# Four-layer backbone kernel: the next unit's scores issued ahead of the inverse's last product, three products placed on other quarters of TensorE, and the last layer's r and g computed for latents only

## The reference

```python
def _rwkv7_step(state, inp):
    r, w, k, v, kk, a = inp
    sa = jnp.einsum("dbhvk,dbhk->dbhv", state, kk)
    state = (state * w[..., None, :] - sa[..., None] * (kk * a)[..., None, :]
             + v[..., None] * k[..., None, :])
    return state, jnp.einsum("dbhvk,dbhk->dbhv", state, r)
...
    r, k, v, g = jnp.einsum("nbtd,nde->nbte", xs[:4], w_rkvg)
...
    _, y = lax.scan(_rwkv7_step, s0, (shared(r), to_scan(decay), to_scan(k_dir),
                                      shared(v), shared(kk), to_scan(iclr)))
    y = y.transpose(1, 2, 0, 3, 4)
    y = y[0] + _seg_flip(y[1], n_ctx, 1)
    if not need_ctx:
        y, r, k, v, g = (a[:, n_ctx:] for a in (y, r, k, v, g))
...
    o = (yn + bonus).reshape(bsz, -1, D_INNER) * jax.nn.silu(g.astype(F32))
```

## Time and profile before

| | |
|---|---|
| median of 3 runs | 6824.17 us |
| profiled execution, its own time | 6829.33 us |
| its span in the trace | 6827.5 us, 212950 instructions |
| TensorE matmul busy | 5819.9 us (85%) |
| VectorE busy | 2964.0 us (43%) |
| ScalarE busy | 2007.9 us (29%) |
| GpSimd busy | 1862.0 us (27%) |
| TensorE's instruction packets (queue q8) | 293, 4.80 MB |
| mean granted TensorE clock | 0.923 |

### The profile page before, as it was taken

The page is one execution under the profiler, slowest core; times in us unless marked ns, Lnnn a source line. Parts: engine busy times, 40 slices in busy tenths (PEclk is TensorE's granted clock), DMA queues, the critical chain, the costliest instruction groups (busy, mean ns, idle before and its releaser), DMA issues. The chain is left out here.

```text
span 6827.5 us, 212950 instructions
## 1 busy us (share of the span) xinstructions
PE 5819.9 (85%) x91944; PEld 3913.5 (57%) x91944; DVE 2964.0 (43%) x6321; ACT 2007.9 (29%) x3323; POOL 1862.0 (27%) x2006
## 2 busy tenths in 40 slices
PE   5999788888887799978897984796999788888887
PEld 4555577777774355445553553543555577777773
DVE  6100366666662233145524368323100366666661
ACT  1000244444440222134312232211000345454440
POOL 4452244443431336000003541000000244434340
PEclk8999899999998899989898987898999999999998
DMA  3222100011002222122122337422111100110002
GB/s 122 90 97 82 42 30 30 30 43 38 30 30 88 115 99 81 39 79 74 50 72 105 100 97 77 135 73 85 69 67 66 41 30 30 43 38 30 30 30 89
DMA packets 196079, 443.13 MB, mean 65 GB/s; under 512 B 24768, under 2 KB 108608, under 8 KB 195648
## 3 DMA queue, kind: packets, MB, share of 16 engines
q1 hardware_dynamic: 160896, 338.58, 16.7%
q10 hardware_dynamic: 34752, 98.61, 3.6%
HBM read 329.14 MB, written 107.97 MB: 64 GB/s over the span
## 5 line engine op out<-in xcount | busy, mean ns | idle before, releaser
L356 PE MATMUL ps<-arena 128*128 128x512 f32 (+1 forms) x4672 | 1713.1, 529 | 73.6 <-DMA arena<-s_w_in 27.6
L356 PEld LDWEIGHTS ps<-arena 128*128 128x128 f32 x4672 | 886.9, 190 | 894.6 <-issue 855.3
L1860 PE MATMUL ps<-arena 64*64 64x64 f32 x35840 | 736.6, 224 | 160.1 <-ACT arena L2245 57.8
L153 POOL TENSOR_TENSOR arena<-arena 128x512 f32<-128x512 f32 (+1 forms) x360 | 331.0, 936 | 1779.3 <-DMA arena<-w_mod 1769.1
L1860 PEld LDWEIGHTS ps<-arena 64*64 64x64 f32 x35840 | 642.5, 136 | 245.6 <-issue 228.8
L2245 ACT COPY arena<-ps 128x512 f32<-128x512 f32 (+1 forms) x880 | 536.0, 630 | 531.7 <-PE ps L1860 521.0
L2388 POOL TENSOR_TENSOR arena<-arena 128x256 f32<-128x256 f32 (+1 forms) x320 | 305.3, 961 | 904.2 <-DVE arena L2609 445.8
L570 PE MATMUL ps<-arena 128*128 128x512 f32 (+1 forms) x1152 | 424.3, 528 | 33.3 <-DMA arena<-na_w_in 33.3
L1621 DVE SCALAR_TENSOR_TENSOR arena<-arena 128x1280 f32<-128x1280 f32 (+2 forms) x128 | 152.5, 1265 | 617.1 <-PE ps L356 502.7
L1685 ACT COPY arena<-ps 128x1280 f32<-128x1280 f32 x64 | 78.4, 1225 | 1105.0 <-PE ps L356 775.0
L2313 POOL MEMSET arena<- 128x1280 f32 (+4 forms) x22 | 15.1, 739 | 1423.7 <-POOLq L83 1423.7
(11 more groups left out here) (258 smaller groups left out, 9730.4 us busy)
## 6 DMA issues: line engine op xcount, KB each, us to landing
arena<-proj SPq DMA_DIRECT2D x158, 640.0 KB, 5.1
proj<-arena ACTq DMA_DIRECT2D x96, 640.0 KB, 3.9
arena<-w_mod SPq DMA_DIRECT2D x96, 512.0 KB, 7.6
arena<-rw_w SPq DMA_DIRECT2D x68, 512.0 KB, 3.6
arena<-xres SPq DMA_DIRECT2D x40, 640.0 KB, 7.0
xres<-arena ACTq DMA_DIRECT2D x24, 640.0 KB, 6.1
arena<-na_w_in SPq DMA_DIRECT2D x24, 512.0 KB, 3.5
arena<-x SPq DMA_DIRECT2D x16, 640.0 KB, 6.6
```

Source lines behind the costliest of these rows:

```text
L153: self.nc.gpsimd.tensor_tensor(out, strip[:, c:c + n, :], self.k.cond[:, c:c + n, s:s + 1].to_broadcast([P, n, P]), ALU.mult)
L356: last = nc.tensor.matmul(k.ps[:, 3 * u + n, 0:b - a], w[:, c * P:(c + 1) * P], src[:, c, a:b], start=(c == 0), stop=(c == KT - 1))
L1860: last = PE.matmul(part_of(out, dst, hh, g, d), part(l, src, hh, g, d), rhs, start=True, stop=True)
```

## The change

- *Scores.* x of the next unit is issued between f4 and f5, xt between f5 and gh (`first_scores`, `turned_scores`). They wait for a new semaphore `kk_ready` (BH and KK made), m for `ops_ready`. The fifth unit issues them too, on old operands, and its result isn't used; the first unit of the next group has its scores issued in the turn, behind step 19. The first pair of all stands before the loop. f5 now goes to `low[2]`, since `low[1]` takes xt.
- *Order in a unit.* On TensorE x2 and x2t come first, then transitions, x4, local outputs, f1. VectorE makes BH ahead of zt's copy, KK behind it, R and the mask of x behind the last `eyed`, the mask of xt before it negates half of gh, and the third mask and KH behind that. ScalarE's decays stand between the copies of f1 and f2, and z's copy ahead of kb's. POOL waits for gh before its first `with_eye`.
- *Quarters.* `product` gets `stay`: with 1, f5's results stay in the half from which they are read, so that f5 uses two quarters and gh, which reads them crosswise, four. w goes over four quarters. The four KK transposes become 16 products with the unit matrix.
- *Last layer.* r and g (n = 0 and 3) are mixed, multiplied, copied and stored for the latents only.
- *Fill.* 147 increments behind layer 0's norm, 217 behind layer 3's.

Cut to its core:

```diff
-NORM_FILL = {0: 19, 3: 148}
+NORM_FILL = {0: 147, 3: 217}
...
+    def tokens_of(n):
+
+        return NCTX if last_layer and n in (0, 3) else 0
...
-                            strip_matmuls(nc, k, u, strips_[:, u, :], xs[n % 2]).then_inc(mm_done[u], 1)
+                            strip_matmuls(nc, k, u, strips_[:, u, :], xs[n % 2], chunks_of(n)).then_inc(mm_done[u], 1)
...
-            def product(out, l, r, t):
+            def product(out, l, r, t, stay=0):
...
-                                src, dst = c ^ (hh & t), c ^ (hh & (t + 1))
+                                src, dst = c ^ (hh & t), c ^ (hh & (t + 1 + stay))
...
-            def window(it, late):
-
-                pe.wait_ge(ops_ready, it + 1)
+            def first_scores():
+                scores(low[0], KK_, BH_).then_inc(x_mm, 1)
+
+            def turned_scores():
+                scores(low[1], BH_, KK_).then_inc(xt_mm, 1)
+
+            def window(it, late, scored):
+
+                pe.wait_ge(xt_ev, it + 1)
                 hold(k, pe)
-                scores(low[0], KK_, BH_).then_inc(x_mm, 1)
-                scores(low[1], BH_, KK_).then_inc(xt_mm, 1)
+                product(low[0], A1, A0, 0).then_inc(x2_mm, 1)
+                product(low[3], A0, A1, 0).then_inc(x2t_mm, 1)
...
                     PE.transpose(bank[7][:, g * P:(g + 1) * P], v_win[:, g * P:(g + 1) * P], k.ident)
                     for d in range(2):
-                        last = PE.transpose(bank[6][:, (g * 2 + d) * P:(g * 2 + d + 1) * P], ops[:, KK_, d, g * P:(g + 1) * P], k.ident)
+                        for hh in range(2):
+                            for c in range(2):
+                                at, col = (2 * g + c) * C, (4 + g * 2 + d) * C
+                                last = PE.matmul(bank[6 + hh][HP[c ^ hh], col:col + C], ops[HP[hh], KK_, d, at:at + C], k.eye2[HP[hh], :],
+                                                 start=True, stop=True)
...
-                                last = PE.matmul(part_of(low[3], c, hh, g, d), part(M1, c, hh, g, d), Vt[HP[c], g, HP[hh]],
+                                last = PE.matmul(part_of(low[3], c ^ hh, hh, g, d), part(M1, c, hh, g, d), Vt[HP[c], g, HP[hh]],
...
                 pe.wait_ge(yz4_ev, it + 1)
+                pe.wait_ge(kk_ready, scored + 2)
+                hold(k, pe)
+                first_scores()
                 pe.wait_ge(f4_ev, it + 1)
                 hold(k, pe)
-                product(low[1], Ya, F, 7).then_inc(f5_mm, 1)
+                product(low[2], Ya, F, 7, 1).then_inc(f5_mm, 1)
+                turned_scores()
 
                 pe.wait_ge(f5_ev, it + 1)
                 hold(k, pe)
-                for hh in range(2):
-                    for g, d, q in pairs:
+                for g, d, q in pairs:
+                    for hh in range(2):
                         for c in range(2):
-                            last = PE.matmul(bank[4 + hh][HP[c], q * P:(q + 1) * P], part(F, c, hh, g, d), RH[HP[c], hh * 4 + q, :],
-                                             start=True, stop=True)
+                            last = PE.matmul(bank[4 + hh][HP[c], q * P:(q + 1) * P], part(F, c ^ hh, hh, g, d),
+                                             RH[HP[c ^ hh], hh * 4 + q, :], start=True, stop=True)
...
                 step(19)
+                pe.wait_ge(kk_ready, e * (NW2 + 1) + (NW2 + 2))
+                hold(k, pe)
+                first_scores()
+                turned_scores()
...
                 for n in range(NW2):
+                    if e or n:
+                        pool.wait_ge(gh_mm, e * NW2 + n)
                     with_eye(n, xt_ev, F[:, 0:M // 2], A1[:, 0:M // 2])
...
                     if n + 2 < NW2:
-                        sums(e, n + 2)
+                        sums_scan(e, n + 2)
+                    if more:
+                        operands_beta(e, n + 1)
                     dve.wait_ge(zt_mm, it)
                     V.tensor_scalar(wide(B1), low[1], -1.0, None, ALU.mult).then_inc(zt_ev, 1)
+                    if more:
+                        operands_kk(e, n + 1)
+                    else:
+                        dve.sem_inc(kk_ready, 1)
...
                     eyed(Ya, low[0]).then_inc(yz4_ev, 1)
-                    if n + 1 < NW2:
-                        operands(e, n + 1)
...
+                    if more:
+                        operands_r(e, n + 1)
+                        mask_scores(e, n + 1)
+                    if n + 2 < NW2:
+                        sums_rest(e, n + 2)
+                    if more:
+                        mask_turned(e, n + 1)
```

More of the change, by code:

```diff
@@ L1636, in _ @@
                 dve.drain()
-                for c in range(KT):
-                    last = mix(0, c, a, b)
-                last.then_inc(xs_part, 1)
+                if a >= tokens_of(0):
+                    for c in range(KT):
+                        last = mix(0, c, a, b)
+                    last.then_inc(xs_part, 1)
             for n in range(1, 6):
@@ L1680, in _, with kept @@
         def _(act):
-            with act.Fori(0, 16) as i:
+            def kept(i, first):
                 for u in range(2):
@@ L2493, in operands_rk, with masked, mask_scores, mask_turned @@
                 dve.drain().then_inc(ops_ready, 1)
-            def operands(e, n, first=False):
-                operands_kk(e, n, first)
-                operands_rk(e, n)
+            def masked(out, in_, mask):
+                return V.tensor_tensor(out.rearrange("p (h g q) -> p h g q", h=2, g=2), in_.rearrange("p h (g q) -> p h g q", g=2),
+                                       flat(mask).unsqueeze(1).unsqueeze(1).to_broadcast([P, 2, 2, 2 * C]), ALU.mult)
+            def mask_scores(e, n):
+                dve.wait_ge(x_mm, e * (NW2 + 1) + (n + 1))
+                hold(k, dve)
+                masked(A0, low[0], k.m_x)
+            def mask_turned(e, n):
+                dve.wait_ge(xt_mm, e * (NW2 + 1) + (n + 1))
+                hold(k, dve)
+                masked(A1, low[1], k.m_xt).then_inc(xt_ev, 1)
+            def mask_rest():
+                masked(NT, low[1], k.m_nt).then_inc(nt_ev, 1)
             def centred(e, banks, c):
@@ L2542, in _ @@
                 kk_unit(0, KK_AHEAD, c)
-            operands(0, 0, True)
+            operands_beta(0, 0, True)
+            operands_kk(0, 0)
+            operands_r(0, 0)
+            mask_scores(0, 0)
+            mask_turned(0, 0)
+            mask_rest()
+            operands_keys(0, 0)
             sums(0, 1)
@@ L2703, in _ @@
                 add_backward(4)
+                mask_turned(e + 1, 0)
+                mask_rest()
+                operands_keys(e + 1, 0)
                 sums(e + 1, 1)
```

100 lines of the change are left out of this document (58 added, 42 removed).

## The result

The changed kernel took 6754.01 us, the median of six runs (6732.09 to 6809.95), against 6823.11 us before (6807.96 to 6831.81); the ratio is 0.9914, with a 95% interval of 0.9888 to 0.9941. It is faster by 0.9%; between the medians stand 69 us, half of the 137 us forecast. Its runs lie 78 us apart, those of before 24 us. The profiled execution is the slowest of them, 6809.95 us (span 6808.1), so its parts are read one by one and not as the median's.

The account below looks back on a forecast made before the run. It took each scan unit as one chain on TensorE with short waits that other engines close. Terms -61 - 32 - 55 + 10.5 + 0.5 = -137 us; 6829.3 - 137 - 5.2 = 6687 us (chance 0.50), own range 6610 to 6760, overall 6610 to 7030.

Parts of the forecast that it names:

- rival A: Layer 0's loop no longer stays loaded: +9.65 us at 32 returns, 6996 us; chance 0.27 in full, 0.07 in part.
- rival B: Scan units do not get shorter, as copies, masks and POOL close waits later: 6765 us; chance 0.08.
- Steady unit: The scan's 64 steady units: -0.95 us each, -61 us in all (-20 to -130).
- scores -1.01: Steady unit: both score products move from the unit's head into idle waits, -1.01 us.
- gh -0.90 and f5 +0.41: Steady unit: gh over four quarters instead of two, -0.90 us; f5 over two instead of four, +0.41 us.
- the mask of xt +0.15: Steady unit: x2 now waits for the mask of xt and comes behind gh's end, +0.15 us.
- the meeting with POOL +0.40: Steady unit: VectorE's KK beside POOL's with_eye, both slow, f3 waiting: +0.40 us, from 0 to +1.0.
- the keys-and-values product: Steady unit: four quarters save 0.41 us on TensorE, counted as nothing; -0.4 if on the path.
- Turns: Turn and first unit of each group: -2.0 us a group, -32 us over 16 (0 to -80).
- Projection: Last layer's r and g for the latents only: 16 shorter strips, -55.0 us (-45 to -60).
- Increments: More increments behind the norms: +10.5 us in layer 3 at 0.152 us each, +0.5 us in layer 0.
- C: Scan units: the gaps give more, -2.0 us a unit, -128 in place of -61, 6620 us; chance 0.08.

Follow-up runs that it names:

- kernel 1: The changed kernel with 97 increments behind layer 0's norm (147 before) and 237 behind layer 3's (217 before): 6714.56 us, ratio 0.9839.
- kernel 2: The changed kernel with 209 increments behind layer 0's norm (147 before) and 155 behind layer 3's (217 before): 7210.92 us, ratio 1.0576.
- kernel 3: The kernel before the change, with 138 increments behind layer 0's norm (19 before) and 29 behind layer 3's (148 before): 7328.76 us, ratio 1.0747.
- kernel 7: As kernel 6, but VectorE computes the rest of the sums ahead of both masks, not between them: 6853.16 us, ratio 1.0048.
- kernel 5: kernel 1 with the old quarters for f5, gh, keys-and-values product and KK transposes, and 293 increments in layer 3: 6716.85 us, ratio 0.9843.
- kernel 9: kernel 1 with VectorE's KK made ahead of BH, in its wait for the transposes: 6708.61 us, ratio 0.9839.
- kernel 4: kernel 1 with the last layer's r and g made for all 1280 tokens, and 109 increments in layer 3: 6754.62 us, ratio 0.9899.
- kernel 6: kernel 1 with both score products of the next unit issued behind gh: 6999.96 us, ratio 1.0265.

## Why the prediction was wrong

**The step that failed** is that the sum takes layer 0's loop as one that stays loaded. The sum has no term for a refetch, although the count beside it put the border at 1711, inside the new body of 1741; with 0.50 against 0.27 for rival A it was the wrong choice. In the profiled execution 6 of the 32 returns fetched the whole loop again, which cost 84.6 us in the steady units (699.3 us, 614.7 in kernel 1) and 28.8 us in layer 0's turns. Moving the border out took 39.5 us off the median, of the 67 us by which 6754 misses 6687.

A itself wasn't right either. It had every return of layer 0 lost, or stops of 2.75 us; what happened is a fourth thing, in which each return is either untouched or lost whole. The counts were right to a few instructions. Missing was a loss by chance, return by return, with only 30 instructions behind the border, which no row of before could tell. How many returns the other five runs lost isn't known; at some 14 us each, their 6732 to 6773 us would fit one to four. The price of a lost return was also low: 9.65 us forecast, 15.3 measured in kernel 2. I took it from a first unit, which waits 2.75 us on "issue" in all; the unit of kernel 2 shown above does so for 9.6 us, 4.35 of them right behind the branch. That 6754 lies in 6610 to 6760 is luck: that range was for a loop that stays loaded, and the refetches of the median run happened to cost less than its margin. The time alone would fit rival B (6765) best; the units of 19.2 us rule it out.

No row showed that a loop over an eighth piece is fetched whole at every return, which A's unit of 28.6 us rests on. The runs showed this in its place: with nothing behind the border none of 64 returns fetched (no packet of q8 in the steady units of the kernel before and of kernel 1), with 30 instructions behind it 6 of 32 did, with 92 63 of 64 (31 in kernel 2, 32 in kernel 3). A lost return waits on "issue" behind the branch, 4.35 us in kernel 2 and 4.39 us in the changed kernel; the returns over seven pieces go back nearly as far and fetched nothing.

**Steady unit: -0.95 us forecast, 19.90 to 19.21 = -0.69 measured** (kernel 1), and -1.0 against the average unit of before (20.2 us). The other 0.3 us is the clock, which the sum had no term for: 11 of the 64 steady units of before took 20.7 to 22.0 us, each with 2.1 to 4.9 us at the lower level, like this one with a granted clock of 0.92. Of the changed kernel's 58 undisturbed units none has any.

```profile
1186.90:1208.40 21.50, 19.57 (x845) 18.36 (x846) 12.94 (x20) 11.78 (x22) 10.54 (x12) 0.92 0.03 6
```

By terms:
- scores -1.01: 0.93 of issue in kernel 7. Right.
- gh -0.90 and f5 +0.41: together -0.05 (kernel 5) and not -0.49. The row's length was right (1.11 us), but I priced gh to its end and not to the start of what waits for it.
- the mask of xt +0.15: 0.29 of wait. It is the reason for the line above, and is counted there.
- the meeting with POOL +0.40: f3's wait grew by 0.26, worth 0.13 (kernel 9). I had both sides slow; KK wasn't (0.68 us), and with_eye took 1.37 us in place of 1.10. The upper end of +1.0, one waiting for the whole of the other, was far off: the two rows stand side by side for 0.41 us only, since KK began 0.27 us earlier.
- the keys-and-values product at nothing: right, a wait of 0.39 us stands in its place.

These terms give -0.93 - 0.05 + 0.13 = -0.85 us against -0.69; the 0.16 between them, and what the rest of the new order did, stay open.

**Turns: -32 us forecast**, -11.5 in kernel 1: -14.5 in layer 0 and +3.0 in layer 3 (seven turns each). I had no row for a turn's saving and took it from the steady unit. This is the second step that failed. The traces of before and of kernel 1 show part of why: over the 14 turns with their first units TensorE's wait for VectorE ahead of the first product behind the turn (4.58 us in the earlier trace rows) fell only from 64.4 to 57.1 us in all, and the one for POOL (27.2 us) gave way to one for VectorE ahead of m (29.6 us). Its waits on "issue" grew from 36.6 to 64.5 us: a first unit's instructions have to be fetched (six packets in the earlier trace rows), and what the new order took off its work came back as waits for them. That the one made the other is my reading and wasn't tested.

**Projection: -55.0**, 55.4 by kernel 4. **Increments: +10.5**, VectorE's wait grew by 11.2; in layer 0 +0.5, by 1.1 (3.62 to 4.76 us). Right.

In sum the kernel without the refetches (kernel 1) gives -106 us, where -137 was forecast: 20 us of the difference are the turns. Rivals B and C fell: units did get shorter, by about what was forecast for them.

## What to carry over

A loop's place in its pieces of instructions is a resource like any other: count the body against the pieces where it really starts, keep it within seven (none of kernel 1's 64 returns fetched, and a border 13 instructions behind the end was enough here), and price up to 15 us (here) for a return over eight. When one edit lengthens a loop, time it at two places of the loop in its piece before judging it. And a faster operation at the end of a chain is worth only the start of its successor: gh lost 0.9 us, x2 began 0.45 us sooner, and f5 had been slowed by as much to make that possible.

## What the hardware showed that I had not expected

A wait of TensorE of 2.65 us was followed by rows at 1.14 us in place of 0.68 (kernel 6), and one of 1.15 us by none (kernel 7). The second and third steady units of each group took 23.9 us in kernel 6 and 20.9 in kernel 7: 1.5 us of sums in VectorE's order became 3.0 us. Runs of the same kernel lie 78 us apart where a return is lost by chance, and 7 to 29 us in the kernels with the border outside. And the 237 increments of kernel 1, which do nothing but move code, make VectorE wait 18.93 us where TensorE has no other work, 15 us more than 63 or 109 of them (4.01 us).
